# A third pair of blocks by seven quarter products in each FFN, and split and sum instructions of 2048 columns on DVE

## The chip, the cores and the metric

One core of a Trainium2 chip runs the whole program: three transformer layers on 256 tokens of width 1024, all in fp32. The metric is the device time of one execution in microseconds. Three runs of the kernel before gave 1045.65, 1046.50 and 1046.73 us, a median of 1046.5 us.

## The reference

Only the feed-forward parts (FFN) are touched by the change. There are three of them, one in each layer, with a hidden width of 2816 (the third has its gate and up weights in two tensors).

```python
D_MODEL = 1024
D_FF = ((8 * D_MODEL // 3 + 255) // 256) * 256      # 2816

def rmsnorm(x, g):
    xf = x.astype(F32)
    y = xf * lax.rsqrt(jnp.mean(xf * xf, axis=-1, keepdims=True) + EPS)
    return (y * g.astype(F32)).astype(x.dtype)

def swiglu(u, w_in, w_out):
    gt, up = jnp.split(u @ w_in, 2, axis=-1)
    return (jax.nn.silu(gt) * up) @ w_out

    for layer in range(DEPTH):
        ...
        h = h + y
        h = h + swiglu(rmsnorm(h, norm_ffn[layer]), ffn_w_in[layer], ffn_w_out[layer])
```

## The kernel before

**Numbers as two parts.** Every fp32 matrix product is done as three TensorE (PE) products of a format with fewer bits: each operand is split into a high part and the rest. For the weights ACT copies the high part (`whi`), then DVE subtracts it from the weight to get the rest (`wlo`). A product is high by high, high by low of the activations (both read `whi`), and last the part that reads `wlo`. So PE can begin a unit once ACT is done with it and needs DVE a little later.

**Units and the ring.** Weights come in units of 512 KB (two DMAs of 256 KB, issued by the SP queue), a unit being 128 partitions x 1024 columns: two 128-row pieces of 512 columns. Six slots form a ring; unit u takes the slot of unit u-6 once PE has used that one (`unit_used`). `wlo` lies in the place of `raw`, the loaded weights. ACT works through the units in order (`feed`, L627), DVE likewise (`feed`, L1172, one instruction of 1024 columns per unit), PE likewise. Each engine's program is one list in a fixed order, and the engines meet only in counting semaphores (`hi_ready`, `lo_ready`, `unit_used`, `hid_ready`, `hid_T`, `hid_hi`, `hid_lo`, `pair_sums`, `pair_copies`).

**An FFN.** The hidden width is cut in 11 blocks of 256. A plain block j has four "up" units (1024 rows of the gate and up weights, 256 + 256 columns) and, later in the order, two "down" units. An up or down unit costs PE 12 matmuls of 512 columns: 2 pieces x 2 token tiles x 3 products. When the up units of a block are done ACT makes SiLU of the gate half, DVE multiplies by the up half (`hid`, L1248), PE transposes (`hid_turn`), ACT and DVE split the transposed block (`brh` L683, `brl` L1253), and the down units follow. `body(j)` on each engine is this step.

**A pair.** Two neighbouring blocks can be taken together: a product of a 2x2 split of the activations (128 tokens x 512 rows) and a 2x2 split of the weights (512 x 512 each), by seven products of quarters (the Winograd form of Strassen's) in place of eight. The seven take 14 units of 6 matmuls, 84 in all, where two plain blocks take 8 units of 12, 96 in all. The price is on the others. The four weight quarters (`b11`, `b12`, `b22`, `b21`, two halves each, called parts) are loaded ahead of time into `work` (`PART_LOADS`, L510) and are not in the ring; DVE makes four sums of weights (`t1` to `t4`, L1288), two instructions of 1024 columns each; ACT and DVE split 14 units and not 8; and DVE adds the products that have to be summed outside the accumulator (`part_sum`, L1340). The sums of activations are made once per FFN. `pair(k, j)` on each engine takes blocks j and j+1, with the down units of block j-1 inside the pair (its units 6 and 7), and after it the four up units of block j+2 (units 16 to 19) and four down units (20 to 23). I number the units within a pair from its first one: unit 0 of a pair is `b` in the code. `PAIRED = (4, 8)`: blocks 4+5 and 8+9 are pairs, and blocks 0, 1, 2, 3, 6, 7 and 10 are plain.

**What a pair's order looks like on DVE** (L1342): split units 0 to 3; split the transposed block (`brl`); split units 4 to 13; `part_sum`; and so on. On PE (L2311): units 0 and 1, the transposes of block j-1, units 2 to 5, down units 6 and 7, units 8 to 15, the transposes of block j, and the up units 16 to 19.

Of the kernel before, what the change touches and what calls it, by code (L numbers as in the profile page):

```python
# [91 lines left out]
_p0 = plan_at("pair", 0, "b11", 0)  # L92
PART_LOADS = {}
for _i, _name in enumerate(PARTS):
    PART_LOADS.setdefault(6 + 2 * _i, []).append((0, _name))
for _i, _name in enumerate(PARTS[:4]):
    PART_LOADS.setdefault(_p0 + 7, []).append((1, _name))
for _i, _name in enumerate(PARTS[4:]):
    PART_LOADS.setdefault(_p0 + 18 + _i, []).append((1, _name))


SUMS = ["a0", "a1", "s1", "s2", "s3", "s4", "l1", "l2", "l3", "l4"]
for _k in range(len(PAIRED)):
    SUMS += [f"{_k}_{_t}_{_i}" for _t in ("t1", "t3", "t2", "t4") for _i in range(2)] + [f"{_k}_{_c}" for _c in ("c22", "c11", "c21")]

# [15 lines left out]
              for i, unit in enumerate(PLAN) if unit[0] == "pair"}  # L121

# [128 lines left out]
def build(nc, D, out):  # L251
    with ExitStack() as ctx:
# [200 lines left out]
        def _(sp):  # L453
# [33 lines left out]
            def load_ffn(u0, gate_w, gate_n0, up_w, up_n0, down_w):  # L487
# [8 lines left out]
                for i, unit in enumerate(PLAN):  # L496
# [104 lines left out]
        def _(act):  # L601
# [34 lines left out]
            def pair_hi(u, n, k, name, half):  # L636
# [3 lines left out]
                else:  # L640
                    act.wait_ge(sem("pair_sums"), sums_done(n, f"{k}_{name}_{half}"))
# [32 lines left out]
            def ffn(n, u0, norm):  # L674
# [25 lines left out]
                def body(j):  # L700
                    b = u0 + plan_at("up", j, 0)
                    feed(b + 5)
                    turn(j + FB * n)
                    if j == 1:
                        for i in range(4):
                            act.wait_ge(sem("pair_sums"), sums_done(n, f"s{i + 1}"))
                            a_(sum_hi(i), F_s[:, i, :, :], ACT.Copy).then_inc(sem("pair_copies"), 1)
                    feed(b + 7)
                    silu(b + 4)

                def pair(k, j):
# [4 lines left out]
                    turn(j + FB * n)  # L716
                    feed(b + 10)
# [36 lines left out]
                turn(FB * (n + 1), 2)  # L754
# [400 lines left out]
        def _(dve):  # L1155
# [88 lines left out]
            def ffn(n, u0, norm, use):  # L1244
# [12 lines left out]
                hidden(2 * FB * n)  # L1257

                def token_sum(name):

                    i = int(name[1])
                    if name[0] == "a":
                        dve.wait_ge(turned_lo, 8 * use + 4 * (i + 1))
                        ins = v_.tensor_tensor(F_a[:, 4 * i:4 * i + 4, :], ath[:, 4 * i:4 * i + 4, :],
                                               atl[:, 4 * i:4 * i + 4, :], ALU.add)
                    else:
                        a11, a12, a21, a22 = (F_a[:, r, c] for c in (slice(0, P), slice(P, S)) for r in (slice(0, 4), slice(4, 8)))
                        x0, x1, op, need = {"s1": (a21, a22, ALU.add, "a1"), "s2": (F_s[:, 0, :, :], a11, ALU.subtract, "s1"),
                                            "s3": (a11, a21, ALU.subtract, "a1"),
                                            "s4": (a12, F_s[:, 1, :, :], ALU.subtract, "s2")}[name]  # L1270
                        dve.wait_ge(sem("pair_sums"), sums_done(n, need))
                        ins = v_.tensor_tensor(F_s[:, i - 1, :, :], x0, x1, op)
                    ins.then_inc(sem("pair_sums"), 1)

                def token_lo(i):
                    dve.wait_ge(sem("pair_copies"), COPIES * n + i + 1)
                    v_.tensor_tensor(sum_lo[:, i, :, :], F_s[:, i, :, :], sum_hi(i), ALU.subtract)\
                        .then_inc(sem("pair_sums"), 1)

                def weight_sum(k, name, i):  # L1280
# [5 lines left out]
                    if x1[0] == "t":  # L1286
                        dve.wait_ge(sem("pair_sums"), sums_done(n, f"{k}_{x1}_{i}"))
# [1675 lines left out]
```

## Time and profile before

| | |
|---|---|
| median of three runs | 1046.5 us |
| profiled execution, its own time | 1046.02 us |
| its span, first to last instruction | 1044.2 us |
| PE busy | 1034.1 us, 99% |
| PE's weight loads (PEld) busy | 841.3 us, 81% |
| DVE busy | 843.2 us, 81% |
| ACT busy | 593.5 us, 57% |
| TensorE clock granted, mean | 0.998 |

The profiled execution is 1.8 us longer than its span and 0.5 us shorter than the median. The busy time of PE is from the start to the modelled end of its matmuls, which overlap, so 99% says that PE is seldom without work, not that it could not go faster. Starts of neighbouring matmuls, 0.227 us apart in the FFNs, are the better measure. In the same way instructions on DVE and ACT overlap a little: six splits of 1024 columns, of 1.22 us each, take 6.89 us in a row, which is 1.13 us from one start to the next.

### The profile page before, as it was taken

To read this page: it belongs to the slowest core of one execution; us is meant where nothing else is said; L and a number is where in the kernel's file an instruction comes from. 1 tells how busy PE (TensorE), PEld (TensorE's weight loads), DVE (VectorE), ACT (ScalarE), POOL (GpSimd) and SP (SyncE) were. 2 spreads that over 40 slices of the span, in tenths; PEclk is the share of its full clock that TensorE was granted. 3 is DMA by queue.
4 is the path that set the end of the run, shared out by engine and by line. 5 is a ranking of instruction groups with operands and counts; after the bars stand their busy time and mean duration, and the time that the engine had idled before them with its cause. 6 is when DMAs were issued, how large, how long until landed. Compare 5 with 4: busy or idle time off the path is not lost.

```text
span 1044.2 us, 13316 instructions
## 1 busy us (share of the span) xinstructions
PE 1034.1 (99%) x4878; PEld 841.3 (81%) x4878; DVE 843.2 (81%) x1366; ACT 593.5 (57%) x897; POOL 21.6 (2%) x30
## 2 busy tenths in 40 slices
PE   8999999999999999999999999999999999999998
PEld 7777778888888888788888888887777888888887
DVE  5877889688777987896977788989978878878784
ACT  5845465565655656655656564538656446465562
POOL 3021000000000000000000000000000000000000
PEclk9999999999999999999999999999999999999999
DMA  8863378373365543683742654444454467739243
GB/s 239 258 194 101 121 227 289 123 253 116 115 208 179 183 143 123 215 285 117 256 155 76 228 170 131 146 158 146 157 160 129 149 190 258 243 121 301 85 152 108
DMA packets 135706, 182.97 MB, mean 175 GB/s; under 512 B 12588, under 2 KB 82730, under 8 KB 135514
## 3 DMA queue, kind: packets, MB, share of 16 engines
q1 hardware_dynamic: 134130, 178.36, 53.0%
q0 software_dynamic: 1104, 3.21, 1.4%
q8 instruction: 39, 0.64, 0.2%
q10 hardware_dynamic: 408, 0.56, 0.2%
q14 instruction: 25, 0.20, 0.1%
HBM read 181.03 MB, written 1.05 MB: 174 GB/s over the span
## 4 chain that ended last, share of the span: by engine, by line
PE 88%; DVE 6%; ACT 2%; SPq 2%; DMA 1%; issue 1%; DVEq 0%
PE ps L2162 13%; PE ps L2167 13%; PE ps L2163 13%; PE ps L2179 7%; PE ps L2180 7%; PE ps L2184 7%; PE ps L2302 4%; PE ps L2304 4%; PE ps L2307 4%; PE ps L2145 3%; PE ps L2147 3%; PE ps L2146 3%; DVE wlo L1169 2%; PE ps L2252 1%; PE ps L2235 1%; DMA raw<-in_a_w_in 1%
## 5 line engine op out<-in xcount | busy, mean ns | idle before, releaser
L1169 DVE TENSOR_TENSOR wlo<-raw,whi 128x1024 fp32r<-128x1024 f32 (+1 forms) x290 | 349.7, 1232 | 34.4 <-ACT whi L625 33.2
L625 ACT ACTIVATE whi<-raw 128x1024 fp32r<-128x1024 f32 (+1 forms) x290 | 295.5, 1053 | 115.3 <-DMA raw<-in_ffn_w_in 33.1
L2162 PE MATMUL ps<-whi,ath 128*128 128x512 f32 (+1 forms) x688 | 275.0, 400 | 3.5 <-ACT whi L625 2.0
L2163 PE MATMUL ps<-whi,atl 128*128 128x512 f32 (+1 forms) x688 | 267.0, 389 | 0.0
L2167 PE MATMUL ps<-wlo,ath 128*128 128x512 f32 (+1 forms) x688 | 183.2, 388 | 0.0
L2162 PEld LDWEIGHTS ps<-whi,ath 128*128 128x128 f32 x688 | 129.6, 188 | 36.8 <-issue 5.9
L2167 PEld LDWEIGHTS ps<-wlo,ath 128*128 128x128 f32 x688 | 128.6, 188 | 27.5 <-DVE wlo L1169 0.6
L2163 PEld LDWEIGHTS ps<-whi,atl 128*128 128x128 f32 x688 | 129.7, 189 | 24.8 <-issue 0.5
L2179 PE MATMUL ps<-whi,brh 128*128 128x512 f32 x272 | 106.6, 392 | 0.0
L2180 PE MATMUL ps<-whi,brl 128*128 128x512 f32 x272 | 105.9, 389 | 0.0
L1183 DVE TENSOR_TENSOR wlo<-work,whi 128x1024 fp32r<-128x1024 f32 x84 | 98.7, 1220 | 4.0 <-ACT whi L642 4.0
L642 ACT ACTIVATE whi<-work 128x1024 fp32r<-128x1024 f32 x84 | 83.9, 1052 | 6.7 <-PE ps L2184 6.7
L2184 PE MATMUL ps<-wlo,brh 128*128 128x512 f32 x272 | 72.7, 389 | 0.0
L1253 DVE TENSOR_TENSOR brl<-ps,brh 128x512 fp32r<-128x512 f32 x33 | 22.8, 690 | 51.8 <-ACT brh L683 51.6
L2179 PEld LDWEIGHTS ps<-whi,brh 128*128 128x128 f32 x272 | 51.1, 188 | 11.2 <-DVE brl L1253 0.5
L2184 PEld LDWEIGHTS ps<-wlo,brh 128*128 128x128 f32 x272 | 51.1, 188 | 10.7
L2180 PEld LDWEIGHTS ps<-whi,brl 128*128 128x128 f32 x272 | 51.1, 188 | 10.3
L1288 DVE TENSOR_TENSOR work<-work 128x1024 f32<-128x1024 f32 x48 | 58.6, 1220 | 0.0
L683 ACT ACTIVATE brh<-ps 128x512 fp32r<-128x512 f32 x33 | 19.6, 594 | 58.6 <-PE ps L2252 58.6
L649 ACT ACTIVATE ath<-ps,gcol 128x256 fp32r<-128x256 f32 x56 | 22.7, 474 | 37.9 <-PE ps L2235 37.9
L1191 DVE SCALAR_TENSOR_TENSOR atl<-ps,gcol,ath 128x256 fp32r<-128x256 f32 x56 | 23.9, 479 | 22.5 <-ACT ath L649 22.5
L2302 PE MATMUL ps<-whi,sum_hi 128*128 128x512 f32 x96 | 38.0, 396 | 0.0
(378 smaller groups left out, 1413.1 us busy)
## 6 DMA issues: line engine op xcount, KB each, us to landing
raw<-in_ffn_w_in SPq DMA_DIRECT2D x112, 256.0 KB, 3.5
raw<-in_w_in SPq DMA_DIRECT2D x104, 256.0 KB, 2.9
raw<-in_ffn_w SPq DMA_DIRECT2D x100, 256.0 KB, 3.4
raw<-in_ffn_w_out SPq DMA_DIRECT2D x88, 256.0 KB, 3.5
work<-in_ffn_w_in SPq DMA_DIRECT2D x64, 256.0 KB, 4.8
raw<-in_a_w_in SPq DMA_DIRECT2D x48, 256.0 KB, 4.2
raw<-in_b_w_in SPq DMA_DIRECT2D x48, 256.0 KB, 3.1
work<-in_ffn_w SPq DMA_DIRECT2D x32, 256.0 KB, 4.9
```

What stands on the lines that cost most here:

```text
L625: a_(unit_view(whi, slot, w), unit_view(raw, slot, w), ACT.Copy).then_inc(hi_ready, 1)
L642: a_(unit_view(whi, u % RING, 512), pair_part(f"{name}_{half}"), ACT.Copy).then_inc(hi_ready, 1)
L1169: v_.tensor_tensor(unit_view(wlo, slot, w), unit_view(raw, slot, w), unit_view(whi, slot, w), ALU.subtract).then_inc(lo_ready, 1)
L1183: v_.tensor_tensor(unit_view(wlo, u % RING, 512), pair_part(f"{name}_{half}"), unit_view(whi, u % RING, 512), ALU.subtract).then_inc(lo_re ...
L1288: v_.tensor_tensor(pair_part(f"{name}_{i}"), pair_part(f"{x0}_{i}"), pair_part(f"{x1}_{i}"), ALU.subtract)\
L2162: mm(ps[bk + apart * t][:, 0:w], ath[:, k, t * P:(t + 1) * P], rh[:, kk, :], start=k == 0, stop=False)
L2163: mm(ps[bk + apart * t][:, 0:w], atl[:, k, t * P:(t + 1) * P], rh[:, kk, :], start=False, stop=False)
L2167: ins = mm(ps[bk + apart * t][:, 0:w], ath[:, k, t * P:(t + 1) * P], rl[:, kk, :], start=False, stop=k == KT - 1)
L2179: mm(o, act_h[:, k, t * P:(t + 1) * P], rh[:, nb, :], start=first, stop=False)
L2180: mm(o, act_l[:, k, t * P:(t + 1) * P], rh[:, nb, :], start=False, stop=False)
L2184: ins = mm(ps[banks[2 * nb + t]][:, :], act_h[:, k, t * P:(t + 1) * P], rl[:, nb, :], start=False, stop=last)
L2302: mm(ps[bank][:, :], hi[:, 2 * i + kk, :], rh[:, kk, :], start=not onto and i + kk == 0, stop=False, skip_group_check=onto)
```

## The change

There are three edits.

1. `PAIRED` becomes `(3, 6, 9)`: blocks 3+4, 6+7 and 9+10 are pairs; 0, 1, 2, 5 and 8 stay plain. An FFN has 84 units and not 78. The last pair has no block behind it and an order of its own: its down unit 6 is one, the other comes as unit 15, `t4` goes ahead of `b22`, and 4 down units end the FFN.
2. DVE splits two neighbouring units of an FFN in one instruction of 2 x 1024 columns (`two_lo`) where both are of one kind, the first is even, and both are in the same call of `feed`. The instruction waits until ACT is done with both, and counts `lo_ready` up by two at its end.
3. DVE's sums of weights and of activations are made of both halves in one instruction (`weight_sum` of 2048 columns), and they stand in other places of DVE's order. The parts of the first pair are loaded at units 6 to 16 (before: 6 to 20), and each later pair's parts within the pair ahead of it, at its unit 7 (four parts) and 18 to 21, as before.

```diff
-PAIRED = (4, 8)
+PAIRED = (3, 6, 9)
 
 PRODUCTS = ("b11", "t3", "t2", "t1", "b21", "b22", "t4")
+LAST_PRODUCTS = ("b11", "t3", "t2", "t1", "b21", "t4", "b22")
...
         if j in PAIRED:
-            half = [("pair", PAIRED.index(j), name, i) for name in PRODUCTS for i in range(2)]
-            plan += half[:6] + [("down", j - 1, k) for k in range(2)] + half[6:]
-            plan += [("up", j + 2, c) for c in range(4)]
-            plan += [("down", j + b, k) for b in range(2) for k in range(2)]
+            last = j + 2 == FB
+            half = [("pair", PAIRED.index(j), name, i) for name in (LAST_PRODUCTS if last else PRODUCTS) for i in range(2)]
+            down = [("down", j - 1, k) for k in range(2)]
+            plan += half[:6] + down[:1] + half[6:] + down[1:] if last else half[:6] + down + half[6:]
+            plan += [("up", j + 2, c) for c in range(4) if j + 2 < FB]
+            plan += [("down", j + b, k) for b in range(2) for k in range(2) if j + b + 1 < FB]
...
             def feed(n):
 
-                for u in range(fed[0], n):
-                    if u in PAIR_UNITS:
+                u = fed[0]
+                while u < n:
+                    kind = [PAIR_UNITS.get(v, (0, 0, 0))[2] for v in (u, u + 1)]
+                    both = u in FFN_UNITS_ALL and u % 2 == 0 and u + 1 < n and kind[0] == kind[1]
+                    if both:
+                        two_lo(u)
+                    elif u in PAIR_UNITS:
                         pair_lo(u, *PAIR_UNITS[u])
                     else:
                         split_lo(u % RING, u + 1, unit_width(u))
+                    u += 1 + both
                 fed[0] = max(fed[0], n)
+
+            def two_lo(u):
+
+                dve.wait_ge(hi_ready, u + 2)
+                at = slice(u % RING, u % RING + 2)
+                src = raw[:, at, 0:UNIT]
+                if u in PAIR_UNITS:
+                    src = pair_both(PAIR_UNITS[u][2]).rearrange("p (s n) -> p s n", s=2)
+                v_.tensor_tensor(wlo[:, at, 0:UNIT], src, whi[:, at, 0:UNIT], ALU.subtract).then_inc(lo_ready, 2)
...
-                def weight_sum(k, name, i):
+                def weight_sum(k, name):
...
-                    v_.tensor_tensor(pair_part(f"{name}_{i}"), pair_part(f"{x0}_{i}"), pair_part(f"{x1}_{i}"), ALU.subtract)\
-                        .then_inc(sem("pair_sums"), 1)
+                    v_.tensor_tensor(pair_both(name), pair_both(x0), pair_both(x1), ALU.subtract).then_inc(sem("pair_sums"), 1)
...
+                def last_pair(k, j, b, copies, hids):
+                    feed(b + 11)
+                    dve.wait_ge(sem("pair_copies"), copies + 3)
+                    part_sum(2, 1)
+                    feed(b + 13)
+                    dve.wait_ge(unit_used, b + 11)
+                    part_sum(0, 3)
+                    feed(b + 14)
+                    hid_of(0, F_part[:, 0, 256:512], hids + 1)
+                    dve.wait_ge(unit_used, b + 13)
+                    part_sum(1, 1)
+                    feed(b + 15)
+                    dve.wait_ge(sem("pair_sums"), sums_done(n, f"{k}_c21"))
+                    hid_of(1, F_part[:, 1, 256:512], hids + 2)
...
                 def pair(k, j):
                     b = u0 + plan_at("pair", k, "b11", 0)
...
                     feed(b + 4)
                     turn(j + FB * n)
+                    feed(b + 8)
+                    weight_sum(k, "t4")
+                    if not more:
+                        last_pair(k, j, b, copies, hids)
+                        return
                     feed(b + 14)
```

The first place is DVE's order in the first pair of the first FFN, units 2 to 13. Before, with `brl` the split of the transposed block, `wlo<-work` a unit of the pair and `wlo<-raw` a down unit:

```order
L1183 TENSOR_TENSOR wlo<-work,whi 128x1024 [waits hi_ready] x3
L1253 TENSOR_TENSOR brl<-ps,brh 128x512 [waits hid_hi]
L1183 TENSOR_TENSOR wlo<-work,whi 128x1024 [waits hi_ready] x2
L1169 TENSOR_TENSOR wlo<-raw,whi 128x1024 [waits hi_ready] x2
L1183 TENSOR_TENSOR wlo<-work,whi 128x1024 [waits hi_ready] x6
L1340 TENSOR_TENSOR work<-work,ps 128x512 [waits pair_copies]
```

And now, where `work<-work` of 2048 columns is the sum `t4`:

```order
L1225 TENSOR_TENSOR wlo<-work,whi 128x2x1024 [waits hi_ready]
L1299 TENSOR_TENSOR brl<-ps,brh 128x512 [waits hid_hi]
L1225 TENSOR_TENSOR wlo<-work,whi 128x2x1024 [waits hi_ready]
L1225 TENSOR_TENSOR wlo<-raw,whi 128x2x1024 [waits hi_ready]
L1332 TENSOR_TENSOR work<-work 128x2048 [waits pair_sums,pair_b21_loaded]
L1225 TENSOR_TENSOR wlo<-work,whi 128x2x1024 [waits hi_ready] x3
L1357 TENSOR_TENSOR work<-work,ps 128x512 [waits pair_copies]
```

Behind `brl` the two splits of units 4 and 5 are one instruction, those of the down units 6 and 7 are one, and the sum `t4` has moved in from the block ahead.

The second place is DVE's order from unit 17 to unit 23, behind the first pair. Before:

```order
L1169 TENSOR_TENSOR wlo<-raw,whi 128x1024 [waits hi_ready]
L1288 TENSOR_TENSOR work<-work 128x1024 [waits pair_b1_loaded]
L1169 TENSOR_TENSOR wlo<-raw,whi 128x1024 [waits hi_ready]
L1288 TENSOR_TENSOR work<-work 128x1024 [waits pair_b1_loaded]
L1253 TENSOR_TENSOR brl<-ps,brh 128x512 [waits hid_hi]
L1169 TENSOR_TENSOR wlo<-raw,whi 128x1024 [waits hi_ready]
L1288 TENSOR_TENSOR work<-work 128x1024 [waits pair_b1_loaded,pair_b22_loaded]
L1169 TENSOR_TENSOR wlo<-raw,whi 128x1024 [waits hi_ready]
```

These are the splits of units 18 to 21 and, between them, halves of the sums `t1` and `t3`. Now:

```order
L1332 TENSOR_TENSOR work<-work 128x2048 [waits pair_b1_loaded]
L1225 TENSOR_TENSOR wlo<-raw,whi 128x2x1024 [waits hi_ready]
L1299 TENSOR_TENSOR brl<-ps,brh 128x512 [waits hid_hi]
L1225 TENSOR_TENSOR wlo<-raw,whi 128x2x1024 [waits hi_ready]
L1332 TENSOR_TENSOR work<-work 128x2048 [waits pair_b1_loaded,pair_b22_loaded]
```

Units 18 and 19 are split together behind `t1`, and 20 and 21 together behind `brl`.

The third place is the last pair, which has no counterpart before; this is DVE from its unit 8 to its unit 14, one unit at a time because the units of one kind no longer begin at an even one (L1229 is such a split, L1357 a `part_sum`):

```order
L1229 TENSOR_TENSOR wlo<-work,whi 128x1024 [waits hi_ready] x3
L1357 TENSOR_TENSOR work<-work,ps 128x512 [waits pair_copies]
L1229 TENSOR_TENSOR wlo<-work,whi 128x1024 [waits hi_ready] x2
L1357 TENSOR_TENSOR work<-work,ps 128x512 [waits unit_used]
L1229 TENSOR_TENSOR wlo<-work,whi 128x1024 [waits hi_ready]
L1353 SCALAR_TENSOR_TENSOR hid<-work,rstd,sil 128x256 [waits sil_ready]
L1357 TENSOR_TENSOR work<-work,ps 128x512 [waits unit_used]
L1229 TENSOR_TENSOR wlo<-work,whi 128x1024 [waits hi_ready]
```

The splits of units 11 and 12 and everything behind them wait for ACT, which copies a finished product between its units 10 and 11.

## Rows read from the trace of the kernel before

**Rows 1.** Windows, most of the first FFN: length, busy by engine (instructions), clock, DMA share, GB/s.
```profile
143.00:368.00 225.00, 224.50 (x1025) 184.98 (x1024) 184.60 (x276) 130.19 (x168) 0.00 (x0) 1.00 0.58 187
```

**Rows 2.** Timeline, PE, first pair and behind: start, duration us, engine, line, operation, count, [idle before].
```profile
197.29 0.61 PE L2307 MATMUL ps<-wlo,ath 128*128 128x512 f32 x2
...
198.65 0.62 PE L2307 MATMUL ps<-wlo,ath 128*128 128x512 f32 x2
...
203.23 0.61 PE L2307 MATMUL ps<-wlo,sum_hi 128*128 128x512 f32 x2
...
206.85 1.07 PE L2184 MATMUL ps<-wlo,brh 128*128 128x512 f32 x4
...
229.57 1.08 PE L2167 MATMUL ps<-wlo,ath 128*128 128x512 f32 x4
```

**Rows 3.** Timeline, DVE, the same pair.
```profile
200.43 0.69 DVE L1253 TENSOR_TENSOR brl<-ps,brh 128x512 fp32r<-128x512 f32 x1 [3.96 <-ACT brh L683]
201.04 2.35 DVE L1183 TENSOR_TENSOR wlo<-work,whi 128x1024 fp32r<-128x1024 f32 x2
...
205.79 1.22 DVE L1169 TENSOR_TENSOR wlo<-raw,whi 128x1024 fp32r<-128x1024 f32 x1 [1.27 <-ACT whi L625]
206.93 6.89 DVE L1183 TENSOR_TENSOR wlo<-work,whi 128x1024 fp32r<-128x1024 f32 x6
...
216.72 0.48 DVE L1336 SCALAR_TENSOR_TENSOR hid<-work,rstd,sil 128x256 f32<-128x256 f32 x1
217.12 1.22 DVE L1183 TENSOR_TENSOR wlo<-work,whi 128x1024 fp32r<-128x1024 f32 x1
```

**Rows 4.** Timeline, ACT, the same stretch.
```profile
199.31 0.60 ACT L698 ACTIVATE work<-ps 128x512 f32<-128x512 f32 x1 [1.66 <-PE ps L2307]
199.80 0.59 ACT L683 ACTIVATE brh<-ps 128x512 fp32r<-128x512 f32 x1
...
204.70 1.06 ACT L625 ACTIVATE whi<-raw 128x1024 fp32r<-128x1024 f32 x1 [2.30 <-DMA raw<-in_ffn_w_out]
...
225.68 1.06 ACT L625 ACTIVATE whi<-raw 128x1024 fp32r<-128x1024 f32 x1 [1.63 <-DMA raw<-in_ffn_w_in]
```

**Rows 5.** Two views: landing of DMAs issued 197.50 to 200.14; then 552.2 to 555.
```profile
DMA to landing us min/median/max: 2.7/3.2/5.0
...
DMA to landing us min/median/max: 2.8/3.3/3.9
```

**Rows 6.** Line L2302, first products of pairs, second and third FFN.
```profile
L2302 PE MATMUL ps<-whi,ath x4: 389/389/389, 486.5 to 488.3; 128*128 128x512 f32 x4
...
L2302 PE MATMUL ps<-whi,ath x12: 389/389/389, 922.9 to 946.9; 128*128 128x512 f32 x12
```

**Rows 7.** Timelines, ACT, second and third FFN, around the first pair.
```profile
494.47 1.06 ACT L625 ACTIVATE whi<-raw 128x1024 fp32r<-128x1024 f32 x1 [1.93 <-DMA raw<-in_ffn_w_out]
...
930.91 1.06 ACT L625 ACTIVATE whi<-raw 128x1024 fp32r<-128x1024 f32 x1 [1.77 <-DMA raw<-in_ffn_w]
...
953.49 1.06 ACT L625 ACTIVATE whi<-raw 128x1024 fp32r<-128x1024 f32 x1 [2.76 <-DMA raw<-in_ffn_w]
...
959.21 1.06 ACT L625 ACTIVATE whi<-raw 128x1024 fp32r<-128x1024 f32 x1 [1.80 <-DMA raw<-in_ffn_w]
```

**Rows 8.** Timeline, PE, third FFN, unit 18 of the first pair.
```profile
956.04 1.08 PE L2167 MATMUL ps<-wlo,ath 128*128 128x512 f32 x4
```

**Rows 9.** Timelines, weight load and matmuls of PE at a wait for DVE.
```profile
146.72 0.19 PEld L2162 LDWEIGHTS ps<-whi,ath 128*128 128x128 f32 x1 [0.56 <-DVE hid L1248]
...
146.19 0.40 PE L2163 MATMUL ps<-whi,atl 128*128 128x512 f32 x1
...
147.06 0.39 PE L2163 MATMUL ps<-whi,atl 128*128 128x512 f32 x1
```

**Rows 10.** Groups by form, DVE: sums of 1024 and of 512 columns.
```profile
L1288 DVE TENSOR_TENSOR work<-work 128x1024 f32<-128x1024 f32 x48 | 58.6, 1220 | 0.0
...
L1272 DVE TENSOR_TENSOR work<-work 128x512 f32<-128x512 f32 x12 | 7.7, 687 | 0.1
```

More of the change, by code:

```diff
@@ L91 @@
 PARTS = [f"{b}_{i}" for b in ("b11", "b12", "b22", "b21") for i in range(2)]
-_p0 = plan_at("pair", 0, "b11", 0)
 PART_LOADS = {}
[L94 to L102, printed above, removed]
-for _k in range(len(PAIRED)):
-    SUMS += [f"{_k}_{_t}_{_i}" for _t in ("t1", "t3", "t2", "t4") for _i in range(2)] + [f"{_k}_{_c}" for _c in ("c22", "c11", "c21")]
+for _k in range(len(PAIRED)):
+    _at = (6, 7, 9, 10, 12, 13, 15, 16)
+    if _k:
+        _b = plan_at("pair", _k - 1, "b11", 0)
+        _at = [_b + _i for _i in (7, 7, 7, 7, 18, 19, 20, 21)]
+    for _i, _name in zip(_at, PARTS):
+        PART_LOADS.setdefault(_i, []).append((_k, _name))
+SUMS = ["a", "s1", "s2", "s3", "s4"]
+for _k in range(len(PAIRED)):
+    SUMS += [f"{_k}_{_c}" for _c in ("t1", "t3", "t2", "t4", "c22", "c11", "c21")]
+SUMS.insert(SUMS.index("0_t1") + 1, "l")
 COPIES = 4 + 3 * len(PAIRED)
@@ L121 @@
               for i, unit in enumerate(PLAN) if unit[0] == "pair"}
+FFN_UNITS_ALL = {u0 + i for u0 in (U_F0, U_F1, U_F2) for i in range(FFN_UNITS)}
 C_COLS = ((768, 512), (1280, 512), (0, 512), (512, 256), (1792, 512), (2304, 512), (2816, 512), (3328, 512))
@@ L1275, in token_lo, with token_sum @@
[L1275 to L1280 removed]
+                feed(u0 + 6)
+                def token_sum():
+                    dve.wait_ge(turned_lo, 8 * use + 8)
+                    v_.tensor_tensor(F_a, ath[:, :, :], atl[:, :, :], ALU.add).then_inc(sem("pair_sums"), 1)
@@ new lines, in token_sums @@
+                def token_sums():
+                    a11, a12, a21, a22 = (F_a[:, r, c] for c in (slice(0, P), slice(P, S)) for r in (slice(0, 4), slice(4, 8)))
+                    s1, s2, s3, s4 = (F_s[:, i, :, :] for i in range(4))
+                    for dst, x0, x1, op, need in ((s1, a21, a22, ALU.add, "a"), (s2, s1, a11, ALU.subtract, "s1"),
+                                                  (s3, a11, a21, ALU.subtract, "a"), (s4, a12, s2, ALU.subtract, "s2")):
+                        dve.wait_ge(sem("pair_sums"), sums_done(n, need))
+                        v_.tensor_tensor(dst, x0, x1, op).then_inc(sem("pair_sums"), 1)
@@ L2325, in pair @@
                     product(b + 4, 0, *s2, onto=True)
+                    if j + 2 == FB:
+                        ffn_down(j, 0, j + FB * n, (b + 6) % RING, b + 7, False, False)
+                        pe.wait_ge(sem("pair_copies"), copies + 2)
+                        product(b + 7, 0, *s1, onto=True)
+                        product(b + 9, 3, *a12)
+                        pe.wait_ge(sem("pair_sums"), sums_done(n, f"{k}_c22"))
+                        product(b + 11, 1, *a22, onto=True)
+                        pe.wait_ge(sem("pair_copies"), copies + 3)
+                        product(b + 13, 0, *s4, onto=True)
+                        hid_turn(hids + 2)
+                        ffn_down(j, 1, j + FB * n, (b + 15) % RING, b + 16, False, False)
+                        for c in range(2):
+                            u = b + 16 + c
+                            if c == 1:
+                                hid_turn(hids + 4)
+                            ffn_down(j + 1, 2 + c, j + 1 + FB * n, u % RING, u + 1, False, False)
+                        return
                     for c in range(2):
@@ L2361, in ffn @@
                 pe.wait_ge(hid_lo, FB * (n + 1))
[L2362 removed]
+                end = [(last, 0, False, False), (last + 1, 1, False, True)]
                 if r < 4:
```

144 lines of the change are left out of this document (64 added, 80 removed).

## The prediction

> **What bounds the kernel now.** I read the page first: PE is busy for 99% of the span, but its matmuls overlap, so that says only that it is never long without work. Then the windows, an FFN at a time: in 225 us of the first FFN PE is busy for 224.5, DVE for 184.6 (82%), ACT for 130, the clock is full [rows 1]. The waits of PE there add up to about 2 us. Then PE's timeline inside a pair, where the load on the other engines is highest: two units of the pair are 1.36 us apart, 6 matmuls of 0.227 us, and that is the same 0.227 us as everywhere [rows 2]. So PE's stream of matmuls bounds all three FFNs, in the pairs too; DVE and ACT have slack, and the reader should ask how much at each point, and not only on average. For that I read the DVE and ACT timelines of the same pair [rows 3, 4] and the landings of the loads [rows 5].
>
> **What is taken away.** A pair costs 84 matmuls and two plain blocks 96. Each FFN gets one more pair: 12 matmuls less in each, 36 in all, at 0.227 us [rows 2] = 8.2 us. Transposes stay 11 per FFN. If nothing waits, the profiled 1046.0 us become 1037.9. That is the ceiling.
>
> **What is added, on DVE.** Of a split of 2 x 1024 columns the trace has none. The two forms [rows 10] give 687 ns for 512 columns and 1220 for 1024, so 533 ns for 512 more; by that line 2048 columns take 1220 + 2 x 533 = 2.29 us. From below it is two starts-to-start without any fixed part, 2.13 us, from above two instructions, 2.44 us. I take 2.29. The Trainium skill (VectorE: DVE Perf Modes, the section on the TRN2 errata) gives 2.291 us for a fp32 tensor_tensor of 2048 columns; no row here has one. In a row, single splits start 1.13 us apart (six in 6.89 us, [rows 3]), so two cost DVE 2.27 us of time and one double 2.20: a merge gives DVE's throughput only 0.07 us per two units. What it costs is latency: the low part of the *first* unit, ready 1.22 us after its start, is now ready 2.29 us after, and the start waits for ACT to be done with the *second* unit. DVE's throughput is no bound before or after (a stretch from one pair to the next is 24 units; 22 of them as eleven doubles, 2 singles, 4 sums, and about 6 us of small work are 41 us, in 204 matmuls or 46 us of PE). So I cost throughput at nothing, and look for each double split whose first unit PE needs soon.
>
> How much PE loses when a low part is late: behind a wait for DVE [rows 9] its weight load, due at 146.19, comes at 146.72, right behind the release, and the matmul after next is at 147.06 where 146.64 was due. A weight load late by 0.53 costs 0.42. The load is due 0.23 ahead of its matmul and goes 0.05 behind the release. So the loss is (ready - due start of the matmul) + 0.17 us, where positive. I put each place through it.
>
> - *Units 4 and 5 of a pair* (behind `brl`). `brl` starts at 200.43 behind a wait of 3.96 us for the transposed block, so DVE can't be earlier; the split starts at 201.04, [rows 3]. Ready now at 203.33 for both. PE's low part of unit 4 is due at 203.23 [rows 2]. Loss 0.27 us, in all 9 pairs: 2.4 us.
> - *Down units 6 and 7.* ACT has unit 7 only at 204.70 + 1.06 = 205.76, its load having landed late, and DVE starts at 205.79 [rows 3, 4]. Before, unit 6 had been split by then. Now both are ready at 208.08; PE wants unit 6 at 206.85 [rows 2], shifted by 0.27. Loss 1.13 us. In the second and third FFN unit 0 of the pair starts at 486.5 and 922.9 [rows 6] and the low part of unit 6 is due 0.91 + 9.56 us later, by the distances of rows 2, so with the shift at 497.24 and 933.64; ACT starts unit 7 at 494.47 and 930.91 [rows 7], both ready 3.38 us later, at 497.85 and 934.29. Losses 0.78 and 0.82. The same issue order (two down units, then four parts) now stands in the first *and* second pair of each FFN, the last pair isn't merged there: 2 x (1.13 + 0.78 + 0.82) = 5.5 us.
> - *Units 18 to 21 behind those two pairs.* First FFN: ACT starts unit 19 at 225.68 [rows 4], ready 229.06, due 229.57 [rows 2]: no loss, but 0.3 us from one. Third FFN: ACT starts 19 and 21 at 953.49 and 959.21 [rows 7]; ready at 956.87 and 962.59; due 956.04 [rows 8] and 5.44 later. Losses 1.00 and 0.28, twice: 2.6 us.
> - *Last pair.* Let X be when PE starts the low part of unit 8. ACT's copy of the product can start at X + 0.66 (199.31 behind 198.65, [rows 2, 4]); then unit 11 on ACT, done at X + 0.66 + 0.49 + 1.06; then on DVE the splits of 11 and 12, a `part_sum` (0.60), split 13, `hid` (0.40, [rows 3]), the last `part_sum`, split 14: ready at X + 2.23 + 3 x 1.13 + 2 x 0.60 + 0.40 + 1.22 = X + 8.44. PE is there at X + 6 x 1.36 = X + 8.16. Loss 0.45 us, three times: 1.4 us.
> - *At nothing:* the activation sums and the weight sums before the first pair (six blocks' worth of lead on DVE at PE's plain pace), and the loads of the first parts, closer together; their cover is the ring, where ACT idles for loads but PE doesn't. If it went, it would cost what rival 3 does. The traffic stays the same, every weight once, and SP issues as many DMAs per FFN: 24 parts and 42 ring units in place of 16 and 50. The DMA engines are busy for 58% of the FFN [rows 1].
>
> Sum: 2.4 + 5.5 + 2.6 + 1.4 = 11.9 against 8.2: 3.7 us more. On the profiled execution 1046.0 + 3.7 = 1049.7; on the median of the runs, 0.5 us above it, 1050.2. I say 1050.
>
> **Forecast, chance 0.43: stalls of the doubled splits outweigh the matmuls.** For it: each place is worked out from a start that the trace has, and down unit 7 was late in all three first pairs. Against: it supposes that loads land in the changed kernel as they did.
>
> **Rival 1, chance 0.27: faster, the loads land earlier.** Everything in the second and third places hangs on the second of two loads. With parts issued behind it a load took up to 5.0 us, without them 3.9 [rows 5]. If it landed 1 us earlier, unit 7 would cost 0.1 at most and units 18 to 21 0.3 at most; what is left is 2.4 + 1.4 and some 0.4: 4.2 - 8.2 = -4.0 us, 1042.5. The point from which it decides is a landing of 4.0 us. The Trainium skill (DMA: Bandwidth & Descriptors, queues, rings and completion order) says that each DMA engine consumes the descriptors of a ring in order. By that rule parts issued behind a load should not hold it up, and its landing would be that of the pair without parts. The trace has 5.0 us against 3.9 for the slowest of four, so I side with the row.
>
> **Rival 2, chance 0.15: no change.** PE's own stalls give the loads and DVE time, so that later places lose less: where unit 6 has cost 0.8, `t4` and the next splits are relieved, and a mean loss of 0.9 us per FFN less makes the sum +1.0, 1047.5. Against it: most loads wait for a slot that PE frees, and move along with its stalls.
>
> **Rival 3, chance 0.15: slower still, places that now just fit.** Unit 18 in the first two FFNs has 0.3 us, and with `t4` in front unit 8 has about 0.1: ready at 205.79 + 2.20 + 2.20 + 2.29 = 212.48, due 20 matmuls behind unit 6's 206.85, at 211.39, plus the 0.27 and 1.13 lost by then, 212.79, of which the 0.17 of the formula goes off. If landings are 0.7 us later than in the trace, each of the six pairs with parts loses some 1.2 us more: +7 us, 1057. For it: parts in all but the last pair mean DMA at its ceiling more often.
>
> **Numbers.** A change within 0.2%, 2.1 us, can't be told from none, so "same" is 1044.4 to 1048.6. The forecast's own range is 1047 to 1053; a fifth of it lies within the bound. Slower: 0.34 of the forecast, 0.15 of rival 3, 0.02 of rival 2 = 0.51. Same: 0.09 of the forecast, 0.12 of rival 2, 0.05 of rival 1 = 0.26. Faster: 0.22 of rival 1 and 0.01 of rival 2 = 0.23. The bounds of the double split (2.13 and 2.44) move the sum by 21 places x 0.15 = 3 us either way. With them 1041.5 to 1056 holds 8 in 10.
>
> **What would show it.** PE waits for `wlo` of the double split (L1225): in nine pairs at unit 4, 0.2 to 0.4 us; in six at unit 6, 0.7 to 1.2 us, with ACT waiting for a DMA just before; three at unit 14 of the last pair. A double split of 2.29 us. Wrong would be: doubles of 2.5 us or more or less than 2.2; no wait at unit 6; waits in the plain blocks ahead of the first pair; or the 36 matmuls missing not being there at all.

## The result, and the profile after

The changed kernel takes 1052.83 us (median of 4 runs, 1052.14 to 1054.29) against 1046.33 for the kernel before (4 runs on the same chip, 1045.65 to 1046.73): 1.0069 times as long, 95% interval 1.0057 to 1.0080, so 6.5 us slower. The execution that the profile shows took 1053.22 us, against 1046.02.

Two lines of the page of the changed kernel: the span, and busy time, share and instructions of each engine.

```profile
span 1051.4 us, 13328 instructions
...
PE 1033.4 (98%) x4842; PEld 832.0 (79%) x4842; DVE 883.3 (84%) x1274; ACT 616.8 (59%) x924; POOL 21.6 (2%) x30
```

The 36 matmuls are gone (4842 are left). PE's share went from 99% to 98%: there is less work, and more waiting in it. The window of rows 1, the same stretch of the changed kernel:

```profile
143.00:368.00 225.00, 221.03 (x998) 179.01 (x996) 195.28 (x234) 134.67 (x174) 0.00 (x0) 1.00 0.57 184
```

[rows 1] had PE busy for 224.50 of 225 us; here it is 221.03, so 4 us of the first FFN are idle. DVE is busier (195.28 us against 184.60), ACT too, and both are still below 90%. What PE's weight loads waited for, in the changed kernel (us in total, times, longest), where the name is a low part of weights; L2220 is PE's line for down units, L2343 for a pair's own products, L2203 for up units and most units outside the FFNs:

```profile
PEld ps L2220 <- DVE wlo L1225: 10.4, 12, 1.4
...
PEld ps L2343 <- DVE wlo L1225: 5.7, 15, 0.6
...
PEld ps L2343 <- DVE wlo L1229: 1.8, 3, 0.6
...
PEld ps L2203 <- DVE wlo L1225: 1.0, 2, 0.6
```

L1225 is the double split, L1229 the single one of a pair's unit. In the kernel before, the products of pairs and of down units waited for no low part at all; the two waits for a low part that it has are outside the FFNs (its L2167 is L2203 here):

```profile
PEld ps L2167 <- DVE wlo L1169: 0.6, 2, 0.4
```

The 18.9 us of the changed kernel are waits of the weight loads, which are due 0.23 us ahead of their matmuls; PE itself loses less, as the timeline shows. The double split by form, and the wide weight sum (busy us, mean ns):

```profile
L1225 DVE TENSOR_TENSOR wlo<-work,whi 128x2048 fp32r<-128x2048 f32 x51 | 115.0, 2284 | 0.4
L1225 DVE TENSOR_TENSOR wlo<-raw,whi 128x2048 fp32r<-128x2048 f32 x47 | 107.5, 2287 | 37.1 <-ACT whi L633 36.9
L1332 DVE TENSOR_TENSOR work<-work 128x2048 f32<-128x2048 f32 x36 | 82.2, 2283 | 0.0
```

The first pair of the first FFN shows both of the main waits. PE's timeline in the changed kernel (start, duration, idle before in brackets):

```profile
186.25 0.39 PE L2340 MATMUL ps<-whi,sum_lo 128*128 128x512 f32 x1
186.85 0.73 PE L2343 MATMUL ps<-wlo,sum_hi 128*128 128x512 f32 x2 [0.21 <-DVE wlo L1225]
...
190.39 0.39 PE L2216 MATMUL ps<-whi,brl 128*128 128x512 f32 x1
191.74 1.20 PE L2220 MATMUL ps<-wlo,brh 128*128 128x512 f32 x4 [0.96 <-DVE wlo L1225]
```

Matmuls follow each other every 0.227 us. Unit 4's low part was due at 186.48 and starts at 186.85; with 0.12 us more until the next matmul group, that place costs 0.49 us. Unit 6's was due at 190.62 and starts at 191.74: 1.24 us with what follows. The chain of waits through this stretch tells why:

```profile
182.57 0.33 SPq L474
...
182.94 5.26 DMA raw<-in_ffn_w_out
...
188.23 1.07 ACT whi L633
...
189.40 2.30 DVE wlo L1225
...
191.74 1.20 PE ps L2220 x4
```

PE waits for a split, that for ACT's rounding of unit 7, that for a load which took 5.3 us. DVE over the same stretch:

```profile
183.91 0.69 DVE L1299 TENSOR_TENSOR brl<-ps,brh 128x512 fp32r<-128x512 f32 x1 [0.90 <-ACT brh L691]
184.52 2.28 DVE L1225 TENSOR_TENSOR wlo<-work,whi 128x2048 fp32r<-128x2048 f32 x1
189.40 2.29 DVE L1225 TENSOR_TENSOR wlo<-raw,whi 128x2048 fp32r<-128x2048 f32 x1 [2.60 <-ACT whi L633]
```

Compare [rows 3]. DVE idles for 2.60 us ahead of the split at 189.40, although unit 6 was ready to be split by 185.86 (ACT below) and DVE was free at 186.80, because one instruction now covers units 6 and 7. ACT:

```profile
182.81 0.58 ACT L706 ACTIVATE work<-ps 128x512 f32<-128x512 f32 x1
183.29 0.59 ACT L691 ACTIVATE brh<-ps 128x512 fp32r<-128x512 f32 x1
184.80 1.06 ACT L633 ACTIVATE whi<-raw 128x1024 fp32r<-128x1024 f32 x1 [0.93 <-DMA raw<-in_ffn_w_out]
188.23 1.06 ACT L633 ACTIVATE whi<-raw 128x1024 fp32r<-128x1024 f32 x1 [2.37 <-DMA raw<-in_ffn_w_out]
```

The loss is all in the FFNs: between the two profiled executions the three stretches that hold them grew by 3.4, 1.0 and 2.75 us, and the rest by 0.2 together.

### The profile page after: what moved, and what is told of

Same layout as the page of the kernel before. It is cut to its first block, busy times and chain, and to the rows that moved or that the text cites. A ratio compares the mean times of both kernels' runs of the same rounds, so it can differ in the third digit from the quotient of the medians.

```text
span 1051.4 us, 13328 instructions
## 1 busy us (share of the span) xinstructions
PE 1033.4 (98%) x4842; PEld 832.0 (79%) x4842; DVE 883.3 (84%) x1274; ACT 616.8 (59%) x924; POOL 21.6 (2%) x30
## 4 chain that ended last, share of the span: by engine, by line
PE 79%; DVE 10%; DMA 6%; ACT 3%; issue 1%; SPq 1%; DVEq 0%; ACTq 0%
PE ps L2198 10%; PE ps L2203 10%; PE ps L2199 10%; PE ps L2220 7%; PE ps L2215 6%; PE ps L2216 6%; PE ps L2343 4%; PE ps L2338 3%; PE ps L2340 3%; DMA raw<-in_ffn_w_out 3%; PE ps L2181 3%; PE ps L2183 3%; PE ps L2182 3%; DMA raw<-in_ffn_w 2%; DVE wlo L1225 2%; DVE wlo L1200 2%
## 5 line engine op out<-in xcount | busy, mean ns | idle before, releaser
L633 ACT ACTIVATE whi<-raw 128x1024 fp32r<-128x1024 f32 (+2 forms) x266 | 271.6, 1052 | 111.8 <-DMA raw<-in_ffn_w_out 32.0
L2198 PE MATMUL ps<-whi,ath 128*128 128x512 f32 (+1 forms) x592 | 237.3, 402 | 3.5 <-ACT whi L633 2.0
L2199 PE MATMUL ps<-whi,atl 128*128 128x512 f32 (+1 forms) x592 | 229.7, 389 | 0.0
L1200 DVE TENSOR_TENSOR wlo<-raw,whi 128x1024 fp32r<-128x1024 f32 (+2 forms) x172 | 208.5, 1239 | 20.5 <-ACT whi L633 19.2
L2203 PE MATMUL ps<-wlo,ath 128*128 128x512 f32 (+1 forms) x592 | 157.5, 388 | 0.2 <-DVE wlo L1225 0.2
L650 ACT ACTIVATE whi<-work 128x1024 fp32r<-128x1024 f32 x126 | 126.1, 1050 | 31.0 <-DVE work L1332 17.9
L1225 DVE TENSOR_TENSOR wlo<-raw,whi 128x2048 fp32r<-128x2048 f32 x47 | 107.5, 2287 | 37.1 <-ACT whi L633 36.9
L2203 PEld LDWEIGHTS ps<-wlo,ath 128*128 128x128 f32 x592 | 110.1, 188 | 24.7 <-DVE wlo L1225 1.0
L1225 DVE TENSOR_TENSOR wlo<-work,whi 128x2048 fp32r<-128x2048 f32 x51 | 115.0, 2284 | 0.4
L1332 DVE TENSOR_TENSOR work<-work 128x2048 f32<-128x2048 f32 x36 | 82.2, 2283 | 0.0
L2220 PE MATMUL ps<-wlo,brh 128*128 128x512 f32 x272 | 74.2, 394 | 5.9 <-DVE wlo L1225 5.7
L2220 PEld LDWEIGHTS ps<-wlo,brh 128*128 128x128 f32 x272 | 50.1, 188 | 20.3 <-DVE wlo L1225 10.4
L2340 PE MATMUL ps<-whi,sum_lo 128*128 128x512 f32 x144 | 56.2, 390 | 0.0
L2343 PE MATMUL ps<-wlo,sum_hi 128*128 128x512 f32 x144 | 45.9, 400 | 1.2 <-DVE wlo L1225 0.6
```

What stands on the lines that cost most here:

```text
L633: a_(unit_view(whi, slot, w), unit_view(raw, slot, w), ACT.Copy).then_inc(hi_ready, 1)
L650: a_(unit_view(whi, u % RING, 512), pair_part(f"{name}_{half}"), ACT.Copy).then_inc(hi_ready, 1)
L1200: v_.tensor_tensor(unit_view(wlo, slot, w), unit_view(raw, slot, w), unit_view(whi, slot, w), ALU.subtract).then_inc(lo_ready, 1)
L1225: v_.tensor_tensor(wlo[:, at, 0:UNIT], src, whi[:, at, 0:UNIT], ALU.subtract).then_inc(lo_ready, 2)
L2198: mm(ps[bk + apart * t][:, 0:w], ath[:, k, t * P:(t + 1) * P], rh[:, kk, :], start=k == 0, stop=False)
L2199: mm(ps[bk + apart * t][:, 0:w], atl[:, k, t * P:(t + 1) * P], rh[:, kk, :], start=False, stop=False)
```

## The experiments

All experiments compute the whole result. Each is compared with the kernel before on the same chip, where that took 1046.07 us (e1 to e4), 1046.52 (e5 to e8) and 1046.52 (e9). The changed kernel's 1052.8 is from its own comparison, where before took 1046.33. A difference between two kernels of different comparisons is therefore uncertain by a few tenths of a us; where that matters the difference is also given with each kernel taken against its own kernel before.

**e1_all_single: the third pair and the wide sums stay, every split is a single one again.**

```diff
-  both = u in FFN_UNITS_ALL and u % 2 == 0 and u + 1 < n and kind[0] == kind[1]
+  both = False
```

> The changed kernel with every split of DVE for one unit again (three pairs per FFN and the sums of 2048 columns stay). Theory (the loss is the late first unit of a double split): the waits at units 4, 6 and 18 to 21 of the pairs, 3.1 + 6.2 + 3.1 us in the changed kernel's trace by PE's starts, go; the three waits at unit 14 of the last pairs (1.4 us) stay. 1052.8 - 12.4 = 1040.4 us, 1039 to 1042. Rival (three pairs give DVE and the DMA engines more than they can do, and the doubles relieve DVE): without doubles DVE has 0.07 us more per two units, so no faster than 1052.8, rather 1054.

Measured 1039.64 us (1039.13 to 1040.00), 0.9938 of before [0.9923, 0.9953]. That is inside the 1039 to 1042 expected. The doubled splits cost 13.2 us (12.9 with each against its own kernel before), and without them the third pair is a gain. Of waits for a low part in the FFNs one group is left; three of its four are at unit 14 of the last pairs and cost PE 0.47 us each, the fourth is one of 0.2 us at unit 14 of a first pair:

```profile
PEld ps L2343 <- DVE wlo L1229: 2.0, 4, 0.6
```

ACT's timeline in e1, then DVE's, then PE's, at the place shown above:

```profile
184.63 1.06 ACT L633 ACTIVATE whi<-raw 128x1024 fp32r<-128x1024 f32 x1 [0.69 <-DMA raw<-in_ffn_w_out]
187.51 1.06 ACT L633 ACTIVATE whi<-raw 128x1024 fp32r<-128x1024 f32 x1 [1.81 <-DMA raw<-in_ffn_w_out]
```

```profile
184.59 2.35 DVE L1229 TENSOR_TENSOR wlo<-work,whi 128x1024 fp32r<-128x1024 f32 x2
186.85 1.22 DVE L1200 TENSOR_TENSOR wlo<-raw,whi 128x1024 fp32r<-128x1024 f32 x1
188.61 1.23 DVE L1200 TENSOR_TENSOR wlo<-raw,whi 128x1024 fp32r<-128x1024 f32 x1 [0.53 <-ACT whi L633]
```

```profile
190.12 1.07 PE L2220 MATMUL ps<-wlo,brh 128*128 128x512 f32 x4
```

Unit 7's load is late here as well, for ACT has it only at 187.51. But unit 6 was split at 186.85 and PE takes it at 190.12 without a wait; unit 7 is split by 189.84 and due 12 matmuls behind unit 6, at 192.84. The late load had 3 us of slack, and the merged split spent it.

**e2_down67_single: only units 6 and 7 of every pair are split singly.**

```diff
+  APART = {... i for u0 in (U_F0, U_F1, U_F2) for k in range(len(PAIRED)) for i in (6,)}
-  both = ... and kind[0] == kind[1]
+  both = ... and kind[0] == kind[1] and u not in APART
```

> The changed kernel with units 6 and 7 alone (the two down units inside the first and second pair of each FFN) split one by one. Theory: the six waits at unit 6 go, 6.2 us: 1046.6 us, 1046 to 1048, since units 8 and 18 to 21 lose what they had gained from PE's earlier stalls. Rival (overload of DVE): PE would wait at the next unit instead, about 1052.

Measured 1047.5 us (1045.04 to 1048.56, 10 runs), 1.0007 [0.9998, 1.0017]: 5.3 us less than the changed kernel, inside the 1046 to 1048 expected. The waits (lines are one or two off where an edit adds lines ahead of them, here by one):

```profile
PEld ps L2344 <- DVE wlo L1226: 5.8, 16, 0.6
PEld ps L2204 <- DVE wlo L1226: 3.3, 6, 0.9
PEld ps L2221 <- DVE wlo L1226: 3.1, 6, 1.1
```

The waits of down units fell from 10.4 us to 3.1, and none of the six that are left is at unit 6: they are all at unit 20. The waits at unit 4 stayed, and those of up units grew from 1.0 to 3.3 us.

**e3_parts_later: the parts that stand behind unit 7's load on the queue wait until PE has used units 0 to 5 of the pair.**

```diff
+  if name == PARTS[0]:
+      sp.wait_ge(unit_used, u0 + plan_at("pair", pair - 1, "b11", 0) + 6)
   sp.wait_ge(lo_ready, ...)
```

> The changed kernel; the four parts loaded at unit 7 of a pair are issued only once PE has used unit 5 of that pair, some 5 us later, so that nothing stands behind the two down units' loads. Theory (the parts behind it hold up the load of unit 7): its slowest landing falls from about 5 us to 3.7 to 4.0, ACT has unit 7 one us earlier, and the wait at unit 6 falls from about 1.0 to 0.1 to 0.3 us: 5 us less, 1048. By the other view (a ring is consumed in order, so what is issued behind a load does not hold it up) the landing and the time stay, 1052.8, or the parts come late for the sums and it is slower.

Measured 1047.05 us (1045.72 to 1048.71, 10 runs), 1.0009 [1.0000, 1.0019]: 5.8 us less than the changed kernel, by another way than e2, with the doubles left as they are; 1048 was expected. Landing of the four DMAs of units 6 and 7 in the first pair, in the changed kernel, then in e3; and SP's queue in each:

```profile
DMA to landing us min/median/max: 2.9/3.3/5.3
```

```profile
DMA to landing us min/median/max: 2.7/3.1/3.7
```

```profile
181.21 2.16 SPq L474 DMA_DIRECT2D raw<-in_ffn_w_out  x4
183.42 5.02 SPq L518 DMA_DIRECT2D work<-in_ffn_w_in  x8
```

```profile
181.48 2.16 SPq L474 DMA_DIRECT2D raw<-in_ffn_w_out  x4
189.27 3.98 SPq L520 DMA_DIRECT2D work<-in_ffn_w_in  x8
```

The four DMAs are the same and stand equally far apart. With the four parts (eight DMAs of 256 KB) issued right behind them the slowest took 5.3 us, with the parts held back 3.7, and ACT begins unit 7 5.4 us after the first of the four was issued instead of 7.0. The first pair of the third FFN, in the changed kernel and in e3, shows the same:

```profile
DMA to landing us min/median/max: 2.7/3.3/5.3
```

```profile
DMA to landing us min/median/max: 2.6/3.0/3.6
```

Over all traces of this case, the slowest of these four DMAs took 4.0 to 5.6 us at the 54 places that have parts right behind it, and 3.5 to 3.7 us at e3's six. So what is issued *behind* a load delays it. It isn't all that does: in the kernel with two pairs the second pair of an FFN has no part behind, and there the slowest took 3.9 and 3.7 us in the second and third FFN, but 4.7 in the first (4.5 in e4), which the prediction had not looked at:

```profile
DMA to landing us min/median/max: 2.9/3.4/4.7
```

The Trainium skill (DMA: Bandwidth & Descriptors, queues, rings and completion order) says that each DMA engine consumes the descriptors of a ring in order, and also that a later one may finish its write before an earlier one. By the first half alone the two landings would be alike, and these runs have them 1.6 us apart; what makes the difference no run here shows.

**e4_two_pairs_doubles: the kernel before, with its two pairs, its order and its sums, and only the doubled splits added.**

```diff
-                for u in range(fed[0], n):
-                    if u in PAIR_UNITS:
+                u = fed[0]
+                while u < n:
...
+                    both = u in FFN_UNITS_ALL and u % 2 == 0 and u + 1 < n and kind[0] == kind[1]
+                    if both:
+                        two_lo(u)
+                    elif u in PAIR_UNITS:
```

(against the kernel before; `two_lo` as in the change)

> The kernel before (two pairs per FFN, its own order and sums), with DVE's double splits alone wherever two units of a kind are fed together: these are units 2 to 13 of the pairs, never 18 to 21. Theory: unit 4 loses 0.3 us in six pairs (1.8), unit 6 loses 1.0 to 1.3 in the three first pairs and 1.1 in the second of the first FFN (4.6), 0.1 in the other two: 6.6 us slower than before, 1053.0, 1051.5 to 1054. Rival (it is the third pair that costs): 1046, the same as before, or a little less.

Measured 1051.7 us (1051.26 to 1051.95), 1.0053 [1.0038, 1.0068]. The doubled splits cost 5.6 us on the old order too, at the lower end of the 5.4 to 7.9 expected, and the waits are of the same kind (here L1198 is the double split, L2203 down units, L2326 a pair's own products):

```profile
PEld ps L2203 <- DVE wlo L1198: 4.3, 6, 1.4
...
PEld ps L2326 <- DVE wlo L1198: 2.4, 6, 0.4
```

So the loss is not one of the third pair. It is larger with three pairs (13.2 us against 5.6), where two pairs of each FFN have parts behind their down loads instead of one. But the two kernels differ in more than that: e4 has six pairs and not nine, no doubles at units 18 to 21, and by PE's starts it loses 1.6 us at its six units 4 and 3.2 us at five of its units 6.

**e5_single_last_pair: e1, and in the last pair of each FFN unit 11 is rounded before the product is copied and split before it is added, not after.** `feed(n)` works up to unit n - 1, and the same edit stands on ACT and on DVE; this is DVE's, in `last_pair`:

```diff
-                    feed(b + 11)
+                    feed(b + 12)
```

> The kernel of all single splits (1039.6 us), and in the last pair of each FFN ACT and DVE take unit 11 ahead of the copy and the sum that stood before it. Theory: the chain from unit 8 to unit 14 gets shorter by the copy (0.5 us) on ACT and a split (1.1 us) on DVE, the three waits at unit 14 (0.47 us each by PE's starts) go: 1039.6 - 1.4 = 1038.2 us. Rival (the wait moves on to unit 15 or to the transposes behind it, since the last pair has too little of PE's work): 1039.6, no change.

Measured 1037.97 us (1037.62 to 1038.76), 0.9919 [0.9907, 0.9932]. It has the lowest median of all kernels here (e8 and e9 can't be told from it), 8.55 us below before with an interval of 7 to 9.7, where the matmuls taken away are worth 8.2. The three waits at unit 14 are gone. The window of rows 1 in e5, three us shorter for the 12 matmuls of this FFN that are gone (2.7 us):

```profile
143.00:365.00 222.00, 221.50 (x1012) 182.56 (x1011) 200.05 (x277) 136.97 (x177) 0.00 (x0) 1.00 0.59 190
```

PE is busy for 221.50 of 222 us, and DVE for 200.05. A DVE that is busy for 90% of an FFN holds nothing up, if its instructions come in time.

**e6_singles_where_due: singles at units 4, 6, 18 and 20 of pairs, doubles elsewhere.** The edit is that of e2 with `for i in (4, 6, 18, 20)`.

> The changed kernel with single splits only at units 4+5, 6+7, 18+19 and 20+21 of the pairs; all other splits stay double. Theory: all of the loss but the 1.4 us in the last pairs hangs on these places, 1052.8 - 12.4 = 1040.4, so the same as with all single ones within 1 us: the doubles that remain neither cost nor gain. Rival (DVE's time is short somewhere): the remaining doubles give DVE 0.07 us each and it is faster than 1039.6; or units 8 and 14, with 0.1 us left by the rows, now lose and it is 1042 or more.

Measured 1041.62 us (1041.22 to 1043.85), 0.9953 [0.9940, 0.9965], 2.0 above e1 (1.5 with each against its own kernel before). The same as e1 within 1 us was expected, and it isn't. The profiled execution is the slowest of the five, 2.2 us above their median. Its waits for low parts of FFN units:

```profile
PEld ps L2344 <- DVE wlo L1226: 3.2, 9, 0.6
...
PEld ps L2344 <- DVE wlo L1230: 1.8, 3, 0.6
...
PEld ps L2221 <- DVE wlo L1226: 1.4, 1, 1.4
```

The nine waits for L1226 at a pair's own products are at units 8 and 14, the places that the rival had named; by PE's starts they cost 1.8 us. At the unit 8 shown here, due at 532.72, the double follows on `t4` without a gap and is ready at 532.80:

```profile
530.51 6.69 DVE L1226 TENSOR_TENSOR wlo<-work,whi 128x2048 fp32r<-128x2048 f32 x3
```

```profile
532.85 0.72 PE L2344 MATMUL ps<-wlo,sum_hi 128*128 128x512 f32 x2
```

The one wait at a down unit is in the second FFN, at unit 22, where the changed kernel had none. PE, then ACT:

```profile
513.95 1.20 PE L2221 MATMUL ps<-wlo,brh 128*128 128x512 f32 x4 [0.99 <-DVE wlo L1226]
```

```profile
509.33 2.17 ACT L634 ACTIVATE whi<-raw 128x1024 fp32r<-128x1024 f32 x2 [2.68 <-DMA raw<-in_ffn_w_out]
```

A load that came 2.68 us after ACT was free cost PE 1.3 us at unit 22: ACT rounds units 22 and 23 one behind the other, and the double can start only after both. So no set of doubles is safe by one trace: each that is left lets its first unit wait for its second.

**e7_unit4_single: singles at unit 4 alone**, again the edit of e2, with `(4,)`.

> The changed kernel with single splits at units 4+5 of each pair alone. Theory, if the losses of the places add up: the nine waits at unit 4 go, 3.1 us by PE's starts: 1049.7. Rival (PE's later arrival at unit 6, whose load is late in any case, takes the gain back in the six pairs that have that wait): only the three last pairs gain, 1 us: 1051.8.

Measured 1051.47 us (1049.71 to 1056.53, 6 runs), 1.0054 [1.0038, 1.0070]; 1.4 us less than the changed kernel (1.5 with each against its own kernel before), where the waits at unit 4 had cost 3.1. That is near the rival's 1051.8 and not the 1049.7 of the theory. The profiled execution took 1053.33 us, 1.9 above the median.

```profile
PEld ps L2221 <- DVE wlo L1226: 11.7, 12, 2.1
...
PEld ps L2204 <- DVE wlo L1226: 3.4, 4, 1.4
...
PEld ps L2344 <- DVE wlo L1226: 1.3, 6, 0.2
```

The wait at the pair's own products went from 5.7 to 1.3 us, that at down units grew from 10.4 to 11.7, and the longest from 1.4 to 2.1. By PE's starts the six units 6 lose 8.1 us here and 6.2 in the changed kernel. PE reaches unit 6 earlier, but the load doesn't come earlier: part of a wait that is removed ahead of a late load goes to the load. This rests on one trace of each kernel. It is also the kernel with the widest spread of runs.

**e8_single_sums_halved: e1, and each wide weight sum is two instructions of 1024 columns.**

```diff
-  v_.tensor_tensor(pair_both(name), ...).then_inc(sem("pair_sums"), 1)
+  for i in range(2):
+      ins = v_.tensor_tensor(pair_part(f"{name}_{i}"), ...)
+  ins.then_inc(sem("pair_sums"), 1)
```

> The kernel of all single splits (1039.6 us) with each sum of weights in two instructions of 1024 columns at the same place. DVE has 36 instructions more, 0.07 us each. Theory (DVE has slack there, latency counts only where the next split is due): 1039.6, within 0.7 us. Rival (DVE is short behind the pairs): each pair loses 0.07 to 0.3 us, 1040.5 to 1042.

Measured 1038.9 us (1038.37 to 1040.22), 0.9929 [0.9917, 0.9941]. Its interval and that of e1 overlap, and its median is the lower one: no gain from the wide sums can be seen. 1039.6 within 0.7 us was expected.

**e9_both: the edits of e5 and e8 together.**

> All single splits, unit 11 taken earlier in the last pair, and each sum of weights in two instructions at the same place: what was best so far, together. If halving the sums does nothing but add 36 x 0.07 us of DVE time in its slack: 1038.0, within 0.5. If the 0.7 us between the kernels with all single splits (1039.6 and 1038.9) is real, because ACT or a split behind the sum gets it sooner: 1037.3. Nothing is left of the 14 us of waits for low parts, so the ceiling of the prediction, 8.2 us under the kernel before, is where it should end.

Measured 1038.52 us (1038.43 to 1039.20), 0.9926 [0.9913, 0.9940], on another chip than e5: no difference from it that can be told, and the upper edge of the 1038.0 within 0.5 us expected. Its waits for low parts in the FFNs add up to 0.2 us.

## Why the prediction was right, and where its terms were off

**The result** lies in the forecast's case, to which it gave a chance of 0.43: slower, by stalls of the doubled splits that outweigh the matmuls; 1052.8 measured, 1050 forecast, with 1047 to 1053 as the forecast's own range. The mechanism is the one that was predicted. The size is less well met than these numbers look: the sum was +3.7 us and the change is +6.5, since a balance of two larger terms (11.9 and 8.2) takes the whole error of each. The terms missed in one direction, so none made up for another.

**What is taken away** (8.2 us) was right as far as the runs can tell: e5, with 0.3 us of waits for low parts left in its pairs, is 8.55 us below before, and e9, with 0.2, 8.0.

**The double split** was estimated at 2.29 us and takes 2.284 to 2.287. That throughput costs nothing was right: e1 runs with all singles, and DVE busier than in the changed kernel, 13 us faster.

**Units 4 and 5**: predicted 0.27 us in nine pairs. Measured 0.26 to 0.28 in the second pairs and 0.27 to 0.29 in the last ones, but 0.49 or 0.50 in the first pair of each FFN: 3.1 us against 2.4. In the first pair ACT was free when PE finished unit 1 in [rows 4] (idle for 1.66 us, copy 0.66 behind PE's start). Now it is rounding weights of 1024 columns then, so its copy starts at 182.81 and not at 182.58 (0.66 behind PE's 181.92), and `brl` and the split are late by that.

**Units 6 and 7**: predicted 5.5 us, measured 6.2 (1.24, 1.02 and 1.29 in first pairs, 1.31, 0.41 and 0.98 in second ones). Here ready - due + 0.17 gives 191.70 - 190.62 + 0.17 = 1.25 against 1.24, so it is the time of arrival that varies, not the price of being late. The last of the four DMAs took 4.7 to 5.0 us in the three first pairs of before and 4.25 to 5.3 in the six of the changed kernel. e2 and e3 show the mechanism from both ends: unmerge the split and the late load is harmless, or hold the parts back and the load isn't late. They give back 5.3 and 5.8 us of the 6.2, each with other waits changed a little too.

**Units 18 to 21** were placed in the third FFN alone, 2.6 us. That was wrong in place: 3.1 us, over all three FFNs. In the first, behind the first pair, ACT has unit 21 only at 217.54, 2.50 us after it was free, and PE loses 1.00 us at unit 20. The assumption that failed is that loads land in the changed kernel as they did in the trace of before; the text had named 0.3 us of room there.

**The last pair**: 0.45 us three times was predicted, 0.47 three times measured. e5 removes it: with each against its own kernel before, e5 is at -8.55 us and e1 at -6.43, 2.1 apart, somewhat more than the 1.4.

**Not in the sum**: between the first FFN and what follows PE waits 0.36 us longer than before for the activations that it transposes. No run is aimed at that. In the traces of e1 and e5 that wait is not there at all, and e1 has one of 0.37 us behind the second FFN, so it isn't tied to the place; its cause stays open.

The places that I can see in the changed kernel's trace add up to 3.1 + 6.2 + 3.1 + 1.4 + 0.4 = 14.2 us; less 8.2 that is +6.0, against +6.5 by the medians and +7.2 in the profiled executions. The rest, 0.5 to 1.2 us, stays open. Against the 11.9 of the prediction three terms were too small by 0.5 to 0.7 each, and the wait behind the first FFN was missing.

**The rivals.** Rival 1 (loads land earlier) needed landings of 4.0 us, and at unit 7 they were 4.25 to 5.3. e3 makes its condition true by hand for units 6 and 7, though not behind the pairs, and gets 1047.05, not 1042.5. Unit 6 then loses nothing; by PE's starts the other places still lose 3.1 us at unit 4, 2.2 behind the pairs and 1.4 in the last pair, 6.7 in all where the rival had 4.2. From 6.7 less 8.2 one would have e3 at 1044.8: the 2 us up to the measured time stay open. Rival 2 (stalls relieve what comes later) is a real effect, since e7 loses at units 6 and behind half of what it gains at unit 4, but it did not bring the sum down: the later places came out above their reckoning, 6.2 for 5.5 and 3.1 for 2.6. Rival 3 saw its places at unit 8 and 18: none at unit 8 in the changed kernel (e6, where PE comes earlier, has three), and 0.24 and 0.49 us at unit 18 in the second and third FFN, far from seven us.

## What to carry to other kernels

Merging two instructions whose inputs arrive at different times makes the first wait for the input of the second, and its result comes later by the second's run time: here 1.07 us and a load's delay, for 0.07 us of DVE time saved. Do it only where the engine's throughput is the bound, which a busy share of 84 to 90% does not show; for that look whether the consumer, here PE, waits.

When a change bundles a gain and a loss, run each alone: the third pair was worth 8.2 us, the doubled splits cost 13, and the sum of the two said only "slower".

## What the runs showed of the hardware

A load of four DMAs of 256 KB lands later when eight more are issued right behind it: the slowest of the four took 4.0 to 5.6 us at 54 places with parts behind (all traces but e3's) and 3.5 to 3.7 at the six of e3. At six places without parts in the traces of before and e4 it took 3.6 to 3.9 four times and 4.5 and 4.7 at the second pair of the first FFN, so what stands behind a load isn't the only cause. That range may be what makes times vary from run to run: kernels whose doubles hang on such loads spread over 2 to 7 us (e2 1045.0 to 1048.6, e3 1045.7 to 1048.7, e7 1049.7 to 1056.5), those with single splits over 0.8 to 1.9 (e1, e5, e8, e9). But that comes from 4 to 10 runs of each, e4, with doubles in another order, spread over 0.7 only, and the kernel before, all single splits, over 2.6 us in 19 runs and 3.1 in 9. So it isn't shown that the doubles widen the spread.

One fp32 subtraction on DVE takes 1.22 us for 1024 columns and 2.28 for 2048, and the next one starts 1.13 and 2.20 us after it in a row. The long form saves 0.07 us and brings its first half 1.07 us later.
